# The triangular inversion of the heads on 32x32 diagonal blocks, with the work around it one level later

## The chip, the cores and the metric

The kernel runs on one core of a Trainium2 chip. It is written for the engines directly: TensorE (PE in the profile), VectorE (DVE), ScalarE (ACT), GpSimd (POOL) and SyncE (SP, which issues the DMAs) each run their own list of instructions in order and meet only through semaphores. The metric is the device time of one execution in microseconds. The kernel before takes 1651.7 us, the median of three runs (1651.15 to 1654.02).

## The reference, cut to what matters

The program is two transformer-like blocks. The change touches one part of the first: the gated delta rule, for 16 value heads in pairs that share a key head, 256 tokens in 4 chunks of 64.

```python
# per head and chunk of 64 tokens; g is a running sum of log decays
decay = jnp.exp(jnp.where(lower, g[..., :, None] - g[..., None, :], -jnp.inf))
L = jnp.where(strict, jnp.einsum('bhncd,bhnsd->bhncs', kb, k) * decay, 0.0)
T = lax.linalg.triangular_solve(eye + L, eye, left_side=True, lower=True, unit_diagonal=True)
u = T @ vb
w = T @ (kb * jnp.exp(g)[..., None])
attn = jnp.einsum('bhncd,bhnsd->bhncs', q, k) * decay
# scan over the chunks
v_new = u_n - w_n @ state
o = q_n @ state + a_n @ v_new
state = state * gl_n + k_n.T @ v_new
# then
o = rmsnorm(o, norm_w) * silu(z)
```

In the kernel a chunk has 128 tokens, so a head has two of them, and `T` is the inverse of a unit lower triangular 128x128 matrix.

## The kernel before, in words

The heads' stage is eight rounds (`GQ = 8`). A round handles one key head, that is two value heads `g`, each with two chunks: four 128x128 matrices are inverted in a round. All four engines run a function `inner(i, f, n)` per round: `i` is the round whose inverse is built, `f` the round before (its recurrence and output are finished in the gaps), `n` the next round (its keys, decays and lower matrices are set up in the gaps).

The inverse grows by doubling. After level `j` the diagonal blocks of size `2^(j+1)` are inverted; a level takes two neighbouring blocks and fills the square below them with `-X2 * L21 * X1`. PE does `level_p` (the product with `L`, line 2410; from level 1 on first a transpose of `X`, line 2406, for the next factor), DVE masks the result out of PSUM into `Pm` (`mask_level`, line 1641; 1638 in level 5), PE does `level_d` (line 2426; 2428 in level 5) and DVE subtracts (`close_level`, line 1652). ACT copies the transposed `X` back (`turned_over`, line 920). All products up to level 4 are over the full 128x128 matrices, whatever the block size, and separately for the two heads `g`; level 5 uses 64x64 products (lines 2413 and 2428). Six levels, 0 to 5, make a round. The start of `X` for the next round is a product of a mask and `L` on DVE (`starts_low` and `starts`, lines 1626 and 1632), transposed on PE (`setup_x0`, line 2385) and copied by ACT (line 938).

Between the levels stand, on PE, the steps 0 to 5 of `finish` (lines 2438 to 2458: the recurrence and output of `f`), `setup_keys` (2364 to 2369), `setup_rows` (2353), `setup_values` (2376), `norm_sums` (2337) and `modulator` (2395). The place of each is written out by hand in the four `inner` functions. `modulator` is something else: a 1 MB tile of `ada_w` (the next block's shift and scale) is loaded in each round into the raw slot 2, scaled and summed by POOL, and summed across partitions by PE.

Weights of the big projections go through four raw slots of 1 MB; ACT makes `w_hi` of a tile (line 738) and DVE `w_lo` (line 1378), in two slots. Right behind the rounds stands the output projection `a_w_out` (`T_AOUT`, line 2515), eight tiles in two halves of four. Its tiles 0 and 1 are loaded before the rounds, tile 2 after the last modulator, tile 3 only when the last output is done (`h_out`), because the raw slot 3 holds `XX`, `LT` and `BV` of the odd rounds.

On PE a plain product in f32 is two instructions in the trace, each a weight load (PEld) and a MATMUL (PE); a transpose is one.

Of the kernel before, what the change touches and what calls it, by code (L numbers as in the profile page):

```python
# [51 lines left out]
def program(nc, x, c, norm_w, ada_w, ada_b, a_w_in, a_conv_w, a_A_log, a_dt_bias, a_norm_w, a_w_out,  # L52
# [4 lines left out]
    with ctx:  # L57
# [112 lines left out]
        def pair(name):  # L170
            return [sem(f"{name}0"), sem(f"{name}1")]

        h_row, h_eg, h_dta, h_dt, h_lt, h_xt, h_xm, h_xT, h_x0, h_vT, h_bv, h_kd = (
            sem("h_row"), sem("h_eg"), sem("h_dta"), sem("h_dt"), sem("h_lt"), sem("h_xt"),
            sem("h_xm"), sem("h_xT"), sem("h_x0"), sem("h_vT"), sem("h_bv"), sem("h_kd"))
        h_p, h_pm, h_d, h_xx = sem("h_p"), sem("h_pm"), sem("h_d"), sem("h_xx")
        h_turn, h_turned = sem("h_turn"), sem("h_turned")
# [23 lines left out]
        MSUM = RAW[2][:, 0, :]  # L201
# [33 lines left out]
        def raw_count(base, i, u):  # L235

            n = base + u
            quads = 48 * ((n - T_WQ) // 4 + 1) if n >= T_WQ else 0
            gates = (0, 0, 16 * GQ, 0)[n % 4] if n >= T_AOUT else 0
            return 16 * i + (16 * (n // 4) + gates + quads)  # L240
# [80 lines left out]
        GBh, DT, KKb, LT, AT, QD, BV, XX, VN, S1h, KD, R1 = ([], [], [], [], [], [], [], [], [], [], [], [])  # L321
        for g_ in range(2):
            for lst, n in ((GBh, 512), (DT, 256), (KKb, 256), (LT, 256), (AT, 256), (QD, 128), (BV, 256),
                           (XX, 512), (VN, 256), (S1h, 128), (KD, 128), (R1, 128)):
                lst.append(temp(n))
        zeroed = at(2048 * (T_AOUT % 4), 2048, RAW01)
        Pm = [[(zeroed[:, 512 * j:512 * j + 512] if j < 4 else GBh[j - 4])[:, 256 * g_:256 * g_ + 256] for g_ in range(2)]
              for j in range(6)]
        LT, AT, QD, BV, XX, KD = [LT], [AT], [QD], [BV], [XX], [KD]
        SQ.append(GBh[0])  # L330
        RN.append(GBh[1])
# [8 lines left out]
        nm1T = LMASK[:, 0:128]  # L340
        lvl = [LMASK[:, 128 * (j + 1):128 * (j + 2)] for j in range(6)]
# [7 lines left out]
        XX.append([at(30720 + 512 * g_, 512) for g_ in range(2)])  # L349

        def left(ap, j, c):

            return ap.rearrange("p (c n h b) -> p c n h b", c=c, h=2, b=2 << j)[:, :, :, 0, :]

        LT.append([at(31744 + 256 * g_, 256) for g_ in range(2)])
        BV.append([at(32256 + 256 * g_, 256) for g_ in range(2)])
        A2 = [ps[0][:, 0:256], ps[1][:, 0:256]]
        A2_FIRST = [ps[2][:, 0:256], ps[3][:, 0:256]]
        B2 = [ps[0][:, 256:512], ps[1][:, 256:512]]
        ROWS = [ps[6], ps[7]]  # L360
        DIAG = two(at(26880, 256))
# [78 lines left out]
        def _(sp):  # L440
# [75 lines left out]
            for u in range(2):  # L516
                load(T_AOUT, 0, u, a_w_out[0, 0:D, :], TW * u)
            with sp.Fori(0, GQ) as i:
                sp.wait_ge(raw_free, i + (8 + N_ADA))
                sp.dma_start(RAW[2], ada_w[1][:, bass.ds(TW * i, TW)].rearrange("(k p) n -> p k n", p=P)).then_inc(raw_in[2], 16)  # L520
            sp.wait_ge(raw_free, 8 + N_ADA + GQ)
            load(T_AOUT, 0, 2, a_w_out[0, 0:D, :], TW * 2)
            for u, read, n in ((0, h_qd, GV), (2, h_vT, GV), (3, h_vT, GV), (1, h_s3, Round(GQ - 1).nth(1, 1, 2, 4))):
                sp.wait_ge(read, n)
                src = ada_w[1][:, 2 * D + TW * u:2 * D + TW * u + TW]
                sp.dma_start(GATEW[u], src.rearrange("(k p) n -> p k n", p=P)).then_inc(gate_in, 16)
            for kh in range(2):
                for u in range(3 if kh == 0 else 0, 4):
                    if kh == 0 and u == 3:
                        sp.wait_ge(h_out, 2 + GV)  # L530
                    load(T_AOUT + 4 * kh, 0, u, a_w_out[0, kh * D:(kh + 1) * D, :], TW * u)
# [69 lines left out]
        def _(pool):  # L601
# [30 lines left out]
            for j in range(6):  # L632
                b = 2 << j
                m = lvl[j].rearrange("p (n h b) -> p n h b", h=2, b=b)[:, :, 0, :]
# [4 lines left out]
            m = nm1T.rearrange("p (n h) -> p n h", h=2)[:, :, 1]  # L639
            keep(m, 0, [[-2, 64]], 1, -1.0, ALU.not_equal)  # L640
# [25 lines left out]
            for i in range(GQ):  # L666
                pool.wait_ge(raw_in[2], 16 * i + 16 * (T_AOUT // 4))
                for kk in range(KC):
                    pool.tensor_tensor(RAW[2][:, kk, :], RAW[2][:, kk, :], condT[:, kk:kk + 1].broadcast_to([P, TW]),
                                       ALU.mult).then_inc(mod_sum, 1)  # L670
                for half, done in ((4, 8), (2, 12), (1, 14)):
                    pool.wait_ge(mod_sum, 15 * i + (24 + done))
                    for kk in range(half):
                        pool.tensor_tensor(RAW[2][:, kk, :], RAW[2][:, kk, :], RAW[2][:, kk + half, :],
                                           ALU.add).then_inc(mod_sum, 1)
# [52 lines left out]
        def _(act):  # L728
# [167 lines left out]
            def setup_keys(r):  # L896
                act.wait_ge(g_k0, r.count(1, 1))
                act.activation(K0, ps[7][:, 0:128], ACT.Copy).then_inc(g_k0s, 1)
                if r.at:
                    act.wait_ge(h_at, r.count(2))  # L900
                act.activation(KQs, two(ps[7][:, 256:512]), ACT.Copy).then_inc(g_kqs, 1)
# [15 lines left out]
            def turned_over(r, j):  # L917
                for g in range(2):
                    act.wait_ge(h_turn, r.nth(g, 1, j - 1, 5))
                    act.activation(XX[r.side][g][:, 256:512], ps[3 + 2 * g][:, 256:512], ACT.Copy).then_inc(h_turned, 1)  # L920
# [13 lines left out]

            def setup_x0(r):
                for g in range(2):
                    act.wait_ge(h_xT, r.nth(g))
                    act.activation(XX[r.side][g][:, 0:256], (A2 if r.at else A2_FIRST)[g], ACT.Copy).then_inc(h_x0, 1)
# [29 lines left out]
            def inner(i, f, n):  # L968
                if f:
                    finish_first(f)  # L970
                turned_over(i, 1)
# [17 lines left out]
                if f:  # L989
                    finish_out(f)  # L990
# [1883 lines left out]
```

## Time and profile before

| | |
|---|---|
| median of the runs | 1651.7 us |
| the profiled execution | 1650.68 us, its span 1649.0 us |
| PE busy | 1594.5 us, 97% |
| DVE, ACT, POOL busy | 68%, 58%, 30% |
| the eight rounds, by the timeline | 198.4 to 360.5 us |
| behind them, the output projection | from 361.3 us |

A busy engine is one with an instruction under way. The profile models the ends of matmuls, so two matmuls that follow each other overlap in it, and the distance of their starts (the pitch) says more than their mean. Idle time is given with what ended it.

### The profile page before, as it was taken

What the parts mean: (1) busy time and instruction counts of PE and PEld (TensorE: products, weight loads), DVE (VectorE), ACT (ScalarE), POOL (GpSimd) and SP (SyncE); (2) the same over time, 40 slices, a digit from 0 to 9 for tenths busy, and PEclk for the clock granted to TensorE, in tenths of its full rate; (3) what the DMA queues carried; (4) which work ended last, traced back from release to release, by engine and by line L of the source; (5) the groups of instructions that cost most, each with busy time, mean ns of one, the idle gap of its engine ahead of it and who ended that gap; (6) DMA issues with size and microseconds to landing.
All of it is one profiled execution on the core that took longest, in us unless ns stands there. A gap on an engine that the chain in (4) does not pass through costs nothing.

```text
span 1649.0 us, 33605 instructions
## 1 busy us (share of the span) xinstructions
PE 1594.5 (97%) x11469; PEld 1482.8 (90%) x11477; DVE 1126.0 (68%) x2361; ACT 949.8 (58%) x1811; POOL 491.9 (30%) x406
## 2 busy tenths in 40 slices
PE   7999999999999999999999999999999999999998
PEld 6899899999898899889999999899999888888886
DVE  3787767755556574586469889889898555555554
ACT  1765566664465554563444444689898555544454
POOL 3000256647000005000037777766666100000000
PEclk9999999999999999999999999999999999999999
DMA  9668211138353245247535555554444556666553
GB/s 292 219 185 279 78 52 52 53 121 257 108 154 103 93 158 179 77 128 184 123 112 169 170 173 166 161 152 141 137 138 132 178 191 192 193 193 196 192 191 128
DMA packets 211818, 255.67 MB, mean 155 GB/s; under 512 B 15911, under 2 KB 193803, under 8 KB 211723
## 3 DMA queue, kind: packets, MB, share of 16 engines
q1 hardware_dynamic: 211723, 254.39, 50.5%
q8 instruction: 62, 1.02, 0.3%
q14 instruction: 33, 0.27, 0.1%
HBM read 253.29 MB, written 1.05 MB: 154 GB/s over the span
## 4 chain that ended last, share of the span: by engine, by line
PE 65%; issue 19%; POOL 9%; DVE 3%; ACT 2%; DMA 2%; SPq 1%; POOLq 0%; another core or an unknown queue 0%; DVEq 0%; ACTq 0%
PE ps L2825 21%; PE ps L2234 14%; PE ps L2807 9%; POOL w_lo L721 8%; PE ps L2795 3%; PE ps L2426 2%; PE ps L2515 2%; PE ps L2410 2%; PE ps L2254 1%; PE ps L2406 1%; DMA arena<-in_ada_w 1%; PE ps L2592 1%; POOL arena L711 0%; PE ps L2612 0%; PE ps L2329 0%
## 5 line engine op out<-in xcount | busy, mean ns | idle before, releaser
L721 POOL TENSOR_TENSOR w_lo<-raw,w_hi 128x1024 fp32r<-128x1024 f32 x128 | 307.6, 2407 | 331.7 <-ACT w_hi L1247 331.4
L2234 PE MATMUL ps<-x_hi,w_hi 128*128 128x256 f32 x1088 | 315.2, 290 | 8.1 <-DVE w_lo L1378 3.0
L2234 PE MATMUL ps<-x_lo,w_hi 128*128 128x256 f32 x1088 | 308.3, 283 | 0.0
L2234 PE MATMUL ps<-x_hi,w_lo 128*128 128x256 f32 x1088 | 308.2, 283 | 0.0
L2193 DVE TENSOR_TENSOR w_lo<-raw,w_hi 128x1024 fp32r<-128x1024 f32 x124 | 152.0, 1225 | 143.3 <-ACT w_hi L1356 143.3
L1356 ACT ACTIVATE w_hi<-raw 128x1024 fp32r<-128x1024 f32 x124 | 131.6, 1061 | 167.9 <-PE ps L2825 167.9
L2234 PEld LDWEIGHTS ps<-x_hi,w_hi 128*128 128x128 f32 x1088 | 209.0, 192 | 14.5 <-issue 5.8
L2234 PEld LDWEIGHTS ps<-x_lo,w_hi 128*128 128x128 f32 x1088 | 209.2, 192 | 1.3 <-issue 1.2
L2234 PEld LDWEIGHTS ps<-x_hi,w_lo 128*128 128x128 f32 x1088 | 209.0, 192 | 0.0
L1247 ACT ACTIVATE w_hi<-raw 128x1024 fp32r<-128x1024 f32 x128 | 134.9, 1054 | 110.3 <-DVE raw L1995 110.2
L2770 PE MATMUL ps<-x_hi,w_hi 128*128 128x256 f32 x576 | 165.1, 287 | 9.5 <-ACT arena L1269 8.2
L1995 DVE STREAM_TRANSPOSE raw<-raw 128x1024 f32<-128x1024 f32 x128 | 158.0, 1235 | 15.6 <-DMA raw<-in_u_experts 13.5
L2770 PE MATMUL ps<-x_lo,w_hi 128*128 128x256 f32 x576 | 162.8, 283 | 0.0
L2770 PE MATMUL ps<-x_hi,w_lo 128*128 128x256 f32 x576 | 162.7, 283 | 0.0
L2825 PE MATMUL ps<-w_hi,x_hi 128*128 128x512 f32 x512 | 157.7, 389 | 1.1 <-DVE x_lo L2183 1.1
L2825 PE MATMUL ps<-w_hi,x_lo 128*128 128x512 f32 x512 | 157.7, 389 | 0.0
L2825 PE MATMUL ps<-w_lo,x_hi 128*128 128x512 f32 x512 | 157.6, 389 | 0.0
L1378 DVE TENSOR_TENSOR w_lo<-arena,w_hi 128x2048 fp32r<-128x2048 f32 (+1 forms) x43 | 97.0, 2256 | 75.7 <-ACT w_hi L738 75.7
L1378 DVE TENSOR_TENSOR w_lo<-raw,w_hi 128x2048 fp32r<-128x2048 f32 (+1 forms) x43 | 97.0, 2255 | 64.1 <-ACT w_hi L738 64.1
L2807 PE MATMUL ps<-x_lo,w_hi 128*128 128x256 f32 x448 | 131.9, 294 | 0.0
L2807 PE MATMUL ps<-x_hi,w_hi 128*128 128x256 f32 x448 | 126.7, 283 | 0.0
L2807 PE MATMUL ps<-x_hi,w_lo 128*128 128x256 f32 x448 | 126.5, 282 | 0.0
(432 smaller groups left out, 3734.9 us busy)
## 6 DMA issues: line engine op xcount, KB each, us to landing
raw<-in_u_experts SPq DMA_DIRECT2D x512, 128.0 KB, 2.6
raw<-in_v_experts SPq DMA_DIRECT2D x128, 512.0 KB, 4.3
arena<-in_ada_w SPq DMA_DIRECT2D x22, 1024.0 KB, 7.8
raw<-in_a_w_in SPq DMA_DIRECT2D x12, 1024.0 KB, 5.8
arena<-in_a_w_in SPq DMA_DIRECT2D x12, 1024.0 KB, 5.5
raw<-in_b_w_in SPq DMA_DIRECT2D x8, 1024.0 KB, 5.5
arena<-in_b_w_in SPq DMA_DIRECT2D x8, 1024.0 KB, 5.5
raw<-in_w_in SPq DMA_DIRECT2D x8, 1024.0 KB, 5.4
```

The source lines that it names most:

```text
L721: pool.tensor_tensor(UTL[e], UT[e % 2], UTH[e].bitcast(F32), ALU.subtract).then_inc(utl_ready, 1)
L1247: act.activation(UTH[e % 4], UT[e % 2], ACT.Copy).then_inc(uth_ready, 1)
L1356: act.activation(VH[u], VRAW[u], ACT.Copy).then_inc(high_ready, 1)
L1378: v.tensor_tensor(WLO[:, slot, 0:k, :], RAW[raw_slot(base, u)][:, 0:k, :], WHI[:, slot, 0:k, :].bitcast(F32), ALU.subtract).then_inc(lo_re ...
L1995: v.transpose(UT[s_].rearrange("p (k a j) -> p a k j", k=KC, a=4), URAW[s_].rearrange("p (a k i) -> p a k i", a=4, k=KC)).then_inc(ut_read ...
L2193: v.tensor_tensor(VL[u], VRAW[u], VH[u].bitcast(F32), ALU.subtract).then_inc(low_ready, 1)
L2234: ins = mm(o[:, b * S:b * S + S], w[:, slot, kk, b * P:b * P + P], xx[:, (kk + turn) % KC, :], start=(kk == 0 and n == 0), stop=(kk == k - ...
L2410: ins = mm(A_[g][:, cc * 128:cc * 128 + 128], lt[:, cc * 128:cc * 128 + 128], xx[:, cc * 128:cc * 128 + 128], start=True, stop=True)
L2770: ins = mm(ps[e % 2][:, 0:S], w[e % 4][:, kk * P:kk * P + P], xx[:, kk, :], start=(kk == 0 and n == 0), stop=(kk == KC - 1 and n == 2))
L2795: ins = mm(GB.rearrange("p (e t) -> p t e", t=4)[:, q, :], OHJ[:, c % 2, q, :], OHI[:, c % 2, q, :], start=True, stop=True, skip_group_che ...
L2807: ins = mm(ps[e % 2][:, 0:S], w[e % 4][:, kk * P:kk * P + P], xx[:, kk, :], start=m == 0, stop=m == 23)
L2825: ins = mm(ps[4 + 2 * t + h][:, :], g[:, u, t * P:t * P + P], w[u][:, 512 * h:512 * h + 512], start=False, stop=False, skip_group_check=True)
```

## The change

Levels 0 to 3 work on the 32x32 diagonal blocks only. The four matrices' diagonal blocks are packed densely: `XC` is `[128, 4, 32]` (partition block `q` of matrix `m` holds that diagonal block), and its transpose `XC_T` is kept beside it by DVE's 32x32 block transpose. A product of a level is 16 small matmuls, one for each matrix `m` and each partition block `q` of 32, with one semaphore at the end for both heads; DVE masks 64 columns for all four matrices in one instruction and subtracts in one. Level 4 uses 32x32 products and writes its results by VectorE into `XPAIR` (64x64 blocks) and `INVT` (the transposed inverse); level 5 uses 64x64 products. ACT spreads the 32x32 blocks into `XPAIR` and `INVT` (`spread`, three parts of two copies). PE's transposes and ACT's copies of them are gone, and so is `setup_x0`; `setup_low` (16 small matmuls with the identity) takes its place. The steps of `finish` and the setup stand one place later. The modulator's tiles alternate between raw slots 2 and 0, the temporaries leave raw slots 1 and 3, and tile 3 of `a_w_out` is loaded before the rounds, tile 2 after the seventh modulator.

```diff
-            with sp.Fori(0, GQ) as i:
-                sp.wait_ge(raw_free, i + (8 + N_ADA))
-                sp.dma_start(RAW[2], ada_w[1][:, bass.ds(TW * i, TW)]...).then_inc(raw_in[2], 16)
+            sp.wait_ge(raw_free, 8 + N_ADA)
+            for i in range(GQ):
+                if i == 1:
+                    sp.wait_ge(lo_ready, tile_no(T_AOUT, 0, 0))
+                elif i:
+                    sp.wait_ge(raw_free, 8 + N_ADA + i - 1)
+                slot = MOD_SLOT[i % 2]
+                sp.dma_start(RAW[slot], ada_w[1][:, TW * i:TW * i + TW]...).then_inc(raw_in[slot], 16)
...
             def mask_level(r, j):
-                for g in range(2):
-                    v.wait_ge(h_p, r.nth(g, 1, j, 6))
...
-                    v.tensor_tensor(left(Pm[j][g], j, 2), left(ps[2 + 2 * g][:, 0:256], j, 2),
-                                    left(lvl[j], j, 1).broadcast_to([P, 2, n, b]), ALU.mult).then_inc(h_pm, 1)
+                v.wait_ge(h_p, r.count(6, j + 1))
+                if j < 4:
+                    n, b = 16 >> (j + 1), 2 << j
+                    mask = lvl[j].rearrange("p (n b) -> p n b", b=b).unsqueeze(1).broadcast_to([P, 4, n, b])
+                    v.tensor_tensor(dense(PC[:, 0:64], j), left(PA[:, 0:128].rearrange("p (m n) -> p m n", m=4), j),
+                                    mask, ALU.mult).then_inc(h_pm, 1)
...
             def close_level(r, j):
...
+                if j < 4:
+                    xx = left(XC, j)
+                    v.tensor_tensor(xx, xx, dense(PBC, j), ALU.subtract).then_inc(h_xx, 1)
+                    v.wait_ge(h_xx, r.count(12, 2 * j + 1))
+                    v.transpose(XC_T, XC).then_inc(h_xx, 1)
...
             def level_p(r, j):
-                        for cc in range(2):
-                            ins = pe.transpose(B_[g][:, 256 + cc * 128:384 + cc * 128], xx[:, cc * 128:cc * 128 + 128], ident)
-                        ins.then_inc(h_turn, 1)
-                    for cc in range(2):
-                        if j < 5:
-                            ins = mm(A_[g][:, cc * 128:cc * 128 + 128], lt[:, cc * 128:cc * 128 + 128],
-                                     xx[:, cc * 128:cc * 128 + 128], start=True, stop=True)
+                if j < 4:
+                    for m, q, g, at_ in diagonal_blocks():
+                        ins = mm(PA[q:q + 32, 32 * m:32 * m + 32], lt[g][q:q + 32, at_:at_ + 32], XC[q:q + 32, m, :],
+                                 start=True, stop=True)
...
             def level_d(r, j):
...
+                if j < 4:
+                    for m, q, g, at_ in diagonal_blocks():
+                        ins = mm(PBC[q:q + 32, 16 * m:16 * m + 16], XC_T[q:q + 32, m, :], PC[q:q + 32, 16 * m:16 * m + 16],
+                                 start=True, stop=True)
...
+            def diagonal_blocks():
+                return [(m, q, m // 2, 128 * (m % 2) + q) for m in range(4) for q in (0, 32, 64, 96)]
```

What PE has at the start of a round (the first two levels, with the steps 0 and 1 of `finish` for the round before), before and now:

```order
L2410 MATMUL ps<-arena 128x128 [waits h_x0]
L2438 MATMUL ps<-arena 128x128 [waits h_x0,h_bv,h_xx] x2
L2426 MATMUL ps<-raw,arena 128x128 [waits h_pm]
L2442 MATMUL ps<-arena 128x128 [waits h_kd,h_c3] x2
L2406 MATMUL ps<-small,arena 128x128 [waits h_xx]
L2410 MATMUL ps<-arena 128x128 x2
L2364 MATMUL ps<-arena 128x128 [waits h_bv,ada_free,g_norm]
```

```order
L2424 MATMUL ps<-arena 32x32 [waits h_xt]
L2424 MATMUL ps<-arena 32x32 x15
L2451 MATMUL ps<-arena 32x16 [waits h_xx,h_xt,h_pm]
L2451 MATMUL ps<-arena 32x16 x15
L2474 MATMUL ps<-arena 128x128 [waits h_bv,h_orn,h_spread,h_xx] x2
L2424 MATMUL ps<-arena 32x32 [waits h_xx]
L2478 MATMUL ps<-arena 128x128 [waits h_kd,h_c3] x2
L2381 MATMUL ps<-arena 128x128 [waits ada_free,g_norm]
```

The first step of `finish` stood between `level_p` and `level_d` of level 0 (line 2438 ahead of 2426); now nothing stands there (2451 right behind 2424), and it comes behind `level_d` (line 2474).

The end of a round on PE, now (levels 4 and 5, the last `finish` step 2494, `setup_low` 2402, the modulator 2410):

```order
L2429 MATMUL ps<-arena 32x32 [waits h_xx]
L2429 MATMUL ps<-arena 32x32 x7
L2456 MATMUL ps<-arena 32x32 [waits h_xx,h_pm]
L2458 MATMUL ps<-arena 32x32 x2
L2494 MATMUL ps<-arena,small 128x256 [waits h_sq] x2
L2402 MATMUL ps<-small,arena 32x32 [waits h_lt]
L2402 MATMUL ps<-small,arena 32x32 x15
L2434 MATMUL ps<-arena 64x64 [waits h_spread,h_xx]
L2410 MATMUL ps<-small,arena 128x1 [waits ada_free,mod_sum]
L2462 MATMUL ps<-arena 64x64 [waits h_spread,h_xx,h_pm]
```

Between `level_p` and `level_d` of level 4 (2429, 2456) nothing stands either; line 2494 stood there before.

## Rows read from the trace of the kernel before

**Rows 1.** The page: the span and PE's busy time.

```profile
span 1649.0 us, 33605 instructions
PE 1594.5 (97%) x11469; PEld 1482.8 (90%) x11477; DVE 1126.0 (68%) x2361; ACT 949.8 (58%) x1811; POOL 491.9 (30%) x406
```

**Rows 2.** Busy time by stretch: two middle rounds, the last but one, the last.

```profile
core 0: us, PE busy (x) PEld busy (x) DVE busy (x) ACT busy (x) POOL busy (x), PEclk, DMA share, GB/s
237.77:258.49 20.72, 20.67 (x173) 19.04 (x174) 15.20 (x44) 13.96 (x44) 12.79 (x19) 1.00 0.17 53
258.49:279.20 20.71, 20.66 (x173) 19.03 (x173) 15.19 (x44) 13.95 (x44) 12.90 (x19) 1.00 0.17 51
320.64:340.50 19.86, 19.81 (x172) 18.77 (x172) 15.17 (x44) 12.91 (x41) 12.90 (x19) 1.00 0.12 41
340.50:359.70 19.20, 17.75 (x153) 16.69 (x152) 11.42 (x32) 15.29 (x32) 11.69 (x15) 1.00 0.16 53
```

**Rows 3.** Groups by line in one round, 237.77 to 258.49 us.

```profile
L2410 PE MATMUL ps<-arena 128*128 128x128 f32 x40 | 6.0, 278 | 0.0
L920 ACT ACTIVATE arena<-ps 128x256 f32<-128x256 f32 x10 | 3.6, 388 | 1.3 <-PE ps L2406 1.3
L1652 DVE TENSOR_TENSOR arena<-arena,ps 128x128 f32<-128x128 f32 (+1 forms) x12 | 3.4, 285 | 3.6 <-PE ps L2426 2.1 <-PE ps L2428 1.5
L2426 PEld LDWEIGHTS ps<-raw,arena 128*128 128x128 f32 x32 | 4.0, 192 | 0.1
L2406 PE MATMUL ps<-small,arena 128*128 128x128 f32 x20 | 3.9, 277 | 0.0
L1641 DVE TENSOR_TENSOR raw<-ps,arena 128x128 f32<-128x128 f32 x8 | 2.2, 286 | 1.1 <-PE ps L2410 1.0
L1605 DVE TENSOR_TENSOR arena<-ps,arena 128x256 f32<-128x256 f32 x2 | 0.8, 420 | 0.4 <-ACT arena L908 0.4
```

**Rows 4.** Timeline: the end of a round and the start of the next.

```profile
256.31 0.44 PE L2406 MATMUL ps<-small,arena 128*128 128x128 f32 x2
256.67 0.44 PE L2413 MATMUL ps<-arena 64*64 64x64 f32 x4
257.05 0.65 PE L2385 MATMUL ps<-small,arena 128*128 128x128 f32 x4
258.49 0.54 PEld L2428 LDWEIGHTS ps<-arena 64*64 64x64 f32 x8 [0.76 <-issue]
258.49 0.68 PE L2428 MATMUL ps<-arena 64*64 64x64 f32 x8
260.43 0.97 PEld L2426 LDWEIGHTS ps<-raw,arena 128*128 128x128 f32 x8
```

**Rows 5.** Line 2428 and, 248 to 250 us, line 2452: durations, starts.

```profile
L2428 PEld LDWEIGHTS ps<-arena x64: 129/135/135, 217.1 to 360.4; 64*64 64x64 f32 x64
L2428 PE MATMUL ps<-arena x64: 218/218/267, 217.1 to 360.5; 64*64 64x64 f32 x64
...
L2452 PEldq EVENT_SEMAPHORE  x2: 51/51/51, 248.7 to 248.8; - x2
```

**Rows 6.** The page: VectorE's 32x32 block transpose elsewhere in the kernel.

```profile
L1995 DVE STREAM_TRANSPOSE raw<-raw 128x1024 f32<-128x1024 f32 x128 | 158.0, 1235 | 15.6 <-DMA raw<-in_u_experts 13.5
```

**Rows 7.** Timeline: PE's first steps of round 0.

```profile
197.42 0.44 PE L2385 MATMUL ps<-small,arena 128*128 128x128 f32 x2 [2.02 <-DVE arena L1632]
198.44 1.35 PE L2410 MATMUL ps<-arena 128*128 128x128 f32 x8
201.00 1.16 PE L2426 MATMUL ps<-raw,arena 128*128 128x128 f32 x8 [1.21 <-DVE raw L1641]
```

**Rows 8.** Behind the rounds: PE's wait (376 to 405 us), the chain, a stretch.

```profile
PE ps L2515 <- DVE w_lo L1378: 2.1, 1, 2.1
...
373.28 6.46 DMA arena<-in_a_w_out
...
384.60:388.00 3.40, 3.40 (x17) 3.40 (x18) 2.38 (x1) 0.09 (x1) 3.40 (x3) 0.50 1.10 348
```

More of the change, by code:

```diff
@@ L526, in _ @@
                 sp.dma_start(GATEW[u], src.rearrange("(k p) n -> p k n", p=P)).then_inc(gate_in, 16)
[L527 to L531, printed above, removed]
+            sp.wait_ge(raw_free, 8 + N_ADA + GQ)
+            for u in range(4):
+                load(T_AOUT + 4, 0, u, a_w_out[0, D:2 * D, :], TW * u)
             for n, tile_ in enumerate(B_ORDER):
@@ L1618, in lowers @@
                     v.wait_ge(h_dt, r.nth(g, 2))
[L1619 removed]
+                    v.wait_ge(h_xm, r.nth(g))
                     v.tensor_tensor(LT[r.side][g], KKb[g], DT[g], ALU.mult).then_inc(h_lt, 1)
[L1622 to L1626 removed]
@@ L1644, in close_level @@
-            def close_level(r, j):
-                for g in range(2):
-                    v.wait_ge(h_d, r.nth(g, 1, j, 6))
-                    if j == 5:
-                        xx = two(XX[r.side][g][0:64, 256:512])[:, :, 64:128]
-                        done = two(ps[3 + 2 * g][0:64, 0:256])[:, :, 0:64]
-                    else:
-                        xx, done = left(XX[r.side][g][:, 0:256], j, 2), left(ps[3 + 2 * g][:, 0:256], j, 2)
-                    v.tensor_tensor(xx, xx, done, ALU.subtract).then_inc(h_xx, 1)
+            def starts(r):
+                v.wait_ge(h_xT, r.count(1, 1))
+                v.tensor_tensor(XC, LOWC.rearrange("p (m n) -> p m n", m=4), bcast(nm1, 4), ALU.mult).then_inc(h_xt, 1)
+                v.wait_ge(h_xt, r.count(3, 1))
+                v.tensor_tensor(XC, XC, bcast(id32, 4), ALU.add).then_inc(h_xt, 1)
+                v.wait_ge(h_xt, r.count(3, 2))
+                v.transpose(XC_T, XC).then_inc(h_xt, 1)
@@ L1700, in inner @@
                 if n:
+                    betas(n)
+                close_level(i, 3)
+                mask_level(i, 4)
+                if n:
                     lowers(n)
@@ L2431, in finish @@
-            def finish(r, step, after=None):
+                lt = LT[r.side]
+                if j == 0:
+                    pe.wait_ge(h_xt, r.count(3, 2))
+                elif j < 5:
+                    pe.wait_ge(h_xx, r.count(12, 2 * j - 1))
+                else:
+                    pe.wait_ge(h_xx, r.count(12, 9))
+                    pe.wait_ge(h_spread, r.count(6, 2))
+                if j < 4:
+                    for m, q, g, at_ in diagonal_blocks():
+                        ins = mm(PA[q:q + 32, 32 * m:32 * m + 32], lt[g][q:q + 32, at_:at_ + 32], XC[q:q + 32, m, :],
+                                 start=True, stop=True)
+                elif j == 4:
+                    for m, q, g, at_ in diagonal_blocks():
+                        if q % 64 == 0:
+                            ins = mm(PA[q + 32:q + 64, 32 * m:32 * m + 32], lt[g][q:q + 32, at_ + 32:at_ + 64], XC[q:q + 32, m, :],
+                                     start=True, stop=True)
+                else:
+                    for m in range(4):
+                        at_ = 128 * (m % 2)
+                        ins = mm(PA[64:128, 64 * m:64 * m + 64], lt[m // 2][0:64, at_ + 64:at_ + 128], XPAIR[0:64, m, :],
+                                 start=True, stop=True)
```

309 lines of the change are left out of this document (155 added, 154 removed).

## The prediction

> **What bounds the kernel now.** I read the page first: PE is busy 97% of the span [rows 1], so PE's time counts nearly everywhere. Then the busy time by stretch over the rounds: a middle round takes 20.7 us and PE is busy for all of it; the last but one 19.9, the last 19.2 with 1.5 us idle [rows 2]. DVE is at 15.2 us of a round, ACT at 14.0, POOL at 12.9, the DMA share at 0.17. So the rounds are bound by PE's own instructions, and a change there is worth what it takes from or adds to PE's sum, the waits that it makes included. The groups by line give PE's counts, the timeline the pitch: eight weight loads of line 2426 take 0.97 us and the last 0.19 (the mean), so the pitch is 0.78 / 7 = 0.111 us for a 128x128 instruction; eight of line 2428, 64x64, take 0.54 and the last 0.135, a pitch of 0.058 [rows 3 to 5]. The pitch halves with the size but for some 4 ns: 64 columns less save 53 ns.
>
> **PE in a middle round, before.** Lines 2410, 2426 and 2406 are 40, 40 (32 in the row, 8 more in level 4) and 20 instructions [rows 3], line 2385 is 4 [rows 4]: 104 at 0.111 = 11.5 us. Levels 5 are 16 at 0.058 = 0.9. Changing between 128 and 64 costs too: from the start of the two transposes at 256.31 to the next 128x128 instruction at 257.05 are 0.74 us, where 2 at 0.111 and 4 at 0.058 make 0.45. That is 0.29 us for going there and back, three times a round (0.9). The rest, 20.7 - 13.3 = 7.4 us, is finish, keys, rows, values, sums and modulator, and stays.
>
> **PE in a middle round, after.** A level from 0 to 3 is 16 products for P and 16 for D, two instructions each: 4 x 64 = 256. Level 4 is 8 and 12 products (40 instructions), setup_low 16 (32). Together 328 small instructions; level 5 is 4 and 4 products, 16 instructions at 0.058 (0.9). No row shows a 32x32 instruction. From above it is bounded by the 64x64 one, 58 ns; from below by the issue: the two semaphore instructions of line 2452 start 0.1 us apart at the row's rounding, and between them in program order stand three products, six weight loads and six matmuls, so PE's sequencer gives out a pair in about 0.15 / 6 = 25 ns or less, and in a standing queue nothing excludes 12 [rows 5]. I take the value that continues the step from 111 to 58: halve 53 once more, 58 - 27 = 31 ns. 328 x 0.031 = 10.2 us.
>
> The round trips between sizes are now nine (finish 0, finish 1 with keys, finish 2, rows, finish 3, finish 4, values, finish 5, modulator with sums); at 0.29 less 0.03 for a shorter first weight load they cost 2.3, and two changes between 32 and 64 without return 0.2.
>
> New waits: between P and D of a level lies one dependent trip. The last matmul ends about 0.19 after its start (0.218 for 64x64 [rows 5]) instead of 0.03, the mask takes about 0.22 on DVE (0.42 for 256 columns of PSUM, 0.286 for 128 [rows 3]: 1.05 ns a column, so 64 columns 0.22), two semaphore steps some 0.1: 0.5 us. Between D and the next P it is the same with the subtraction. Before, the other head's products covered it; now both heads end with one semaphore. Where something stands in the gap it is covered (finish 0 to 3 are 4 x 0.111 + 0.26 = 0.7 us each, rows and values as much). Nothing stands between P and D of level 0 and of level 4: 1.0 us a round. The block transpose (1235 ns for 1024 columns [rows 6], so about 0.2 for 128) is needed only for D and lies beside P.
>
> Sum: 10.2 + 0.9 + 7.4 + 2.5 + 1.0 = 22.0 us, 1.3 more than 20.7. In six of the rounds (1 to 6): +7.8 us.
>
> In the last round nothing stands for the next: 296 small ones 9.2, 0.9, finish and modulator 4.3, seven trips 1.8 and 0.2, and four open gaps 2.0: 18.4 against 19.2, -0.8. In round 0 finish is missing: 10.2 + 0.9 + 3.1 + 1.3 + 3.0 (six open gaps) = 18.5; before, 19.3 from 198.44 to the next round's start, 1.2 of it the wait for DVE's memsets [rows 7]: -0.8.
>
> **The other engines.** DVE loses lines 1652, 1641, 1638, 1626, 1632 (about 9 us a round by the first two rows and their like) and gains some 5 us; ACT loses twelve copies of 0.388 (4.7) and gains six of about 0.28 (1.7). Neither becomes the bound at 22 us. The order on each was walked through: `normed` (2 x 0.6 us) before `close_level` 5 delays only D of level 0, one us later than it ends; `lowers` (1.2 us) stands before the closing of level 4, whose results PE needs after finish 5 and setup_low, 2 us later. `starts` waits for ACT's spreads, queued behind setup_v; behind it wait the level-5 mask and the modulator's copy; ACT is through with about 1 us to spare. If that cover is gone it costs 1 us a round. POOL's modulator (12.9 us a round) gets a second slot and stays hidden.
>
> **Ahead of the rounds.** PE waited 2.0 us for `starts_low` and `starts` [rows 7]. Now: lowers start 0.4 earlier (no memset before), low takes 1.0, two DVE operations 0.6, semaphores 0.2; the first P at about 197.2 instead of 198.4: -1.2.
>
> **Behind the rounds.** PE waits 2.1 us for `w_lo` of tile 3, whose DMA was issued at 373.28 when the last output was done, and took 6.46; right behind, for 3.4 us, the granted clock is 0.50, that is 1.2 instead of 2.4 GHz, after the wait: 1.7 us of work lost [rows 8]. Tiles 2 and 3 are now loaded long before, and the DMA queue of that stretch is 2 MB shorter. What is late next is tile 4 (its load now follows the gate tiles at about 364, needed at 388): hidden. -3.8 us; bounds 0 and -4.
>
> **Total.** 7.8 - 0.8 - 0.8 - 1.2 - 3.8 = +1.2 us. The profiled execution took 1650.7, its span 1649.0, and stands 1.0 below the median; 1650.7 + 1.2 = 1651.9, in terms of the median 1652.9. I forecast 1652: no change that can be told (a measurement of this kernel tells about 0.2%, 3.3 us).
>
> The sum hangs on the pitch: 328 x 8 = 2600 instructions, so each ns is worth 2.6 us. 58 ns give +70, 17 ns -37.
>
> **Rules against and for.** The row of line 2452 bears on a rule of the Trainium skill (TensorE: Matmul & The Clock Gate, section "Wait — 56ns, not 53.3ns?"): with hardware decode off the sequencer spends about 62 ns per matmul. Six matmuls would take 0.37 us, and the two semaphore instructions start 0.1 apart, so the trace speaks against it; by that rule alone the sum would be 328 x 31 ns = 10 us a round higher, 1733. The same section gives a floor of about 25 ns from start to start, by which the sum would be 16 us lower, an estimate from that page.
>
> **Rival 1: the blocks overlap (30%).** Consecutive small products use other partitions for input and output (q = 0, 32, 64, 96). If PE loads one block's weights while another's product runs, only the two instructions of one product stay in line, and a product costs about 31 + 4 ns: 17 ns an instruction. A round is then 22.0 - 328 x 0.014 = 17.4 us, with DVE and ACT near 13 still below it; eight rounds give -37, the time is 1616. For it: the order of the blocks makes it possible. Against: no product in this trace runs beside another. The Trainium skill (TensorEngine Tiling (Array Packing), section "Tiling Modes") says that different tiles load weights and multiply in parallel; no row here shows it.
>
> **Rival 2: a small instruction costs as much as a 64x64 one (16%).** Its place is the pair of weight load and matmul, 58 ns in line 2428. From about 33 ns on it makes the kernel slower by more than 0.2%; at 58 the rounds take 30.7 us and the time is 1722; at 40, 1676. For it: 58 is the shortest pitch of a pair in the trace. Against: it continues the line from 111 in proportion, as no floor would.
>
> **Rival 3: the clock (4%).** PE's gaps now come twice a level. If the granted clock fell to 1.2 GHz as after the 2.1 us wait [rows 8], PE's 21 us a round would double: over 1800. Against: 2.0 and 1.2 us of waits at 197 to 201 left it at full speed, and no gap here is over 1 us.
>
> **Rival 4: open gaps cost more (10%).** DVE's and ACT's queues close up and add 1 us in each round: 1661.
>
> **Chances.** The forecast's own case 40%, with a range of 1643 to 1662 for a pitch of 28 to 35 ns, both signs and no change about equally; rival 1 30%, rival 2 16%, rival 4 10%, rival 3 4%. Faster by over 0.2%: 0.30 + 0.15 = 0.45; within 0.2%: 0.16; slower 0.39. The range 1612 to 1678 takes in the overlap and pitches up to 40 ns; it leaves out the upper part of rival 2 and the clock.
>
> **What the changed profile would show.** The pitch of the 32x32 lines 2424 and 2451: 31 ns, a burst of 32 in 1.0 us; with overlap 0.55 us; with a floor 1.9. A round of 22 us with PE idle for 0.4 to 0.5 us twice (at lines 2451 in level 0 and 2456). PEclk at 1.00. No wait at line 2515 and no half clock behind the rounds. DVE and ACT at 12 to 13 us a round. I am wrong if a burst is much shorter or longer than 1.0 us, if PE waits for ACT's spreads, or if the stretch behind the rounds keeps its 3.8 us.

## The result, and the profile after

The changed kernel takes 1624.5 us (median of 4 runs, 1621.4 to 1628.8) against 1652.1 for the kernel before (1651.2 to 1654.0): ratio 0.983, 95% interval 0.981 to 0.986. In a second comparison on one chip it was 1624.3 (5 runs) against 1650.0, ratio 0.983 [0.982, 0.985]. I had forecast 1652 and no change; the kernel is 1.7% faster. The time is inside the range of 1612 to 1678, but the mechanism is not mine. It is that of rival 1, stronger than I had priced it, with part of the gain given back, so that the time lies inside the range is no merit of my sum.

The page of the changed kernel: span, PE, granted clock, instruction packets. These answer to [rows 1].

```profile
span 1619.6 us, 37025 instructions
PE 1554.8 (96%) x13269; PEld 1429.3 (88%) x13269; DVE 1109.9 (69%) x2304; ACT 932.7 (58%) x1763; POOL 493.4 (30%) x405
PEclk9999979899999999999999999999999999999999
q8 instruction: 76, 1.25, 0.3%
```

PE's time fell by 40 us, the span by 29.4. PEclk has a 7 and an 8 in the slices of the rounds, where the page of the kernel before has 9 throughout. The busy time by stretch (columns as in [rows 2]): round 1, round 2, a hole, a middle round, the last. Rounds are cut at the first product of line 2410.

```profile
209.13:228.75 19.62, 18.88 (x399) 14.70 (x398) 10.15 (x33) 10.69 (x35) 12.41 (x20) 0.72 0.18 56
228.75:244.08 15.33, 14.39 (x400) 11.24 (x398) 13.05 (x38) 11.80 (x39) 13.18 (x20) 1.00 0.23 72
244.08:260.67 16.59, 14.53 (x400) 11.35 (x398) 13.03 (x38) 11.79 (x39) 13.16 (x20) 1.00 0.20 66
260.67:275.95 15.28, 14.34 (x400) 11.23 (x398) 13.04 (x38) 11.79 (x39) 13.17 (x20) 1.00 0.24 73
306.51:325.82 19.31, 16.10 (x350) 13.42 (x348) 10.85 (x29) 12.91 (x30) 8.85 (x13) 0.65 0.67 217
```

Four of the middle rounds take 15.28 to 15.33 us, against 20.7 before [rows 2]. Round 1 and the last are 4 us longer, at a mean clock of 0.72 and 0.65. The trace has the half clock from 203.1 to 220.2 us (17.1 us, over rounds 0 and 1) and from 308.9 to 322.6 (13.7 us, in the last). Timeline of PE in a middle round, then the broken burst of the 16.59 us round:

```profile
277.45 0.68 PE L2462 MATMUL ps<-arena 64*64 64x64 f32 x8
278.05 0.45 PE L2424 MATMUL ps<-arena 32*32 32x32 f32 x32
279.05 0.44 PE L2451 MATMUL ps<-arena 32*32 32x16 f32 x32 [0.54 <-DVE arena L1653]
279.45 0.69 PE L2474 MATMUL ps<-arena 128*128 128x128 f32 x4
280.07 0.45 PE L2424 MATMUL ps<-arena 32*32 32x32 f32 x32
...
288.81 0.21 PE L2456 MATMUL ps<-arena 32*32 32x32 f32 x1 [0.39 <-DVE arena L1656]
```

```profile
250.22 0.37 PE L2451 MATMUL ps<-arena 32*32 32x16 f32 x22
251.72 0.29 PE L2451 MATMUL ps<-arena 32*32 32x16 f32 x10 [1.13 <-issue]
```

A burst of 32 takes 0.45 us, of which the last instruction is 0.19. From its first start to its last the trace has 263 ns, 263 / 31 = 8.5 ns from one to the next, where 64x64 instructions still stand 58 ns apart. The two open gaps are there as forecast, 0.54 and 0.39 us. Groups by line in the same round (what answers to [rows 3]):

```profile
L2424 PE MATMUL ps<-arena 32*32 32x32 f32 x128 | 1.8, 194 | 0.0
L1664 DVE TENSOR_TENSOR arena<-arena,ps 128x64 f32<-128x64 f32 x4 | 0.9, 218 | 1.3 <-PE ps L2451 1.3
L1653 DVE TENSOR_TENSOR arena<-ps,arena 128x64 f32<-128x64 f32 x4 | 0.8, 212 | 0.1
```

The mask and the subtraction on 64 columns take 0.21 and 0.22 us, as worked out from the wider ones. The hole of 1.13 us in the broken burst has no releaser: the burst stops after 22 of its 32. A second one, in the last round, is 0.3 us. The page counts 76 instruction packets, against 62 before, and the transfers of the trace speak for late instructions: a packet of 16 KB landed at 250.24 us, 1.5 us before the burst went on. In the profiles of this kernel and its edits below, PE has 34 such holes of 0.3 to 2.8 us in the rounds, and every one ends 1.2 to 1.6 us after a 16 KB instruction packet has landed. (Two kinds that recur at the same place with no such packet are left out: 0.33 us ahead of line 2372, and the one behind the last D, of which more below.)

By milestones in the two traces, after minus before: the first P is 2.1 us earlier (196.32 against 198.44 [rows 7]). The eight rounds, from there to the last D, take 130.1 us against 161.3 (-31.2), and from the last D to the end of the output projection the time is 2.0 shorter. That is -35.3. Then 2.8 us are lost at 650 us. These are the same instructions with the same wait ahead in both kernels, after and before:

```profile
650.79 0.80 PE L2628 MATMUL ps<-arena 128*128 128x128 f32 x2 [2.18 <-DVE arena L1828]
654.59 0.41 PE L2253 MATMUL ps<-x_lo,w_hi 128*128 128x256 f32 x1
```

```profile
686.06 0.49 PE L2592 MATMUL ps<-arena 128*128 128x128 f32 x2 [2.18 <-DVE arena L1809]
688.03 0.28 PE L2234 MATMUL ps<-x_lo,w_hi 128*128 128x256 f32 x1
```

Behind an equal wait of 2.18 us one execution fell to half clock (6.8 us long) and the other did not. The same wait stands in all eleven further profiles below, and ten of them fall there (for 3.4 or 6.8 us), only `no_gap` does not; with one profile of the kernel before, the record doesn't tell an effect of the change from chance. The remaining +3.2 us lie in the expert stretch, where PE waits 9.7 us for ScalarE instead of 8.2. That stretch differs by some us between the profiles of every kernel below, none of which touches it, and I don't put it down to the change.

### The profile page after: what moved, and what is told of

It is laid out like the page before. It is cut to its first block, busy times and chain, and to the rows that moved or that the text cites. A ratio compares the mean times of both kernels' runs of the same rounds, so it can differ in the third digit from the quotient of the medians.

```text
span 1619.6 us, 37025 instructions
## 1 busy us (share of the span) xinstructions
PE 1554.8 (96%) x13269; PEld 1429.3 (88%) x13269; DVE 1109.9 (69%) x2304; ACT 932.7 (58%) x1763; POOL 493.4 (30%) x405
## 4 chain that ended last, share of the span: by engine, by line
PE 72%; DVE 11%; issue 5%; DMA 4%; ACT 4%; SPq 2%; DVEq 0%; ACTq 0%
PE ps L2253 22%; PE ps L2861 22%; PE ps L2843 10%; PE ps L2831 3%; DMA raw<-in_u_experts 3%; PE ps L2273 2%; PE ps L2551 2%; DVE raw L2014 2%; SPq L580 2%; PE ps L2628 1%; DVE w_lo L1396 1%; PE ps L2451 1%; DMA arena<-in_ada_w 1%; DVE arena L2067 1%; PE ps L2648 1%
## 5 line engine op out<-in xcount | busy, mean ns | idle before, releaser
L2253 PEld LDWEIGHTS ps<-x_hi,w_hi 128*128 128x128 f32 x1088 | 209.1, 192 | 15.3 <-issue 6.0
L2014 DVE STREAM_TRANSPOSE raw<-raw 128x1024 f32<-128x1024 f32 x128 | 158.3, 1237 | 17.1 <-DMA raw<-in_u_experts 15.8
```

The costliest lines, as they stand in the source:

```text
L2014: v.transpose(UT[s_].rearrange("p (k a j) -> p a k j", k=KC, a=4), URAW[s_].rearrange("p (a k i) -> p a k i", a=4, k=KC)).then_inc(ut_read ...
L2253: ins = mm(o[:, b * S:b * S + S], w[:, slot, kk, b * P:b * P + P], xx[:, (kk + turn) % KC, :], start=(kk == 0 and n == 0), stop=(kk == k - ...
```

## Experiments

All are edits of the changed kernel. Unless said otherwise, the kernel before, run beside them on the same chip, took 1650 to 1651 us.

**Four products on one block in a row.**

```
-  return [... for m in range(4) for q in (0, 32, 64, 96)]
+  return [... for q in (0, 32, 64, 96) for m in range(4)]
```

> The changed kernel, but the 16 products of a burst stand in another order: four on the same 32 partitions in a row, then the next block, where they now go from block to block. Nothing is added. Theory (four blocks work beside each other: the profile of the changed kernel has a matmul every 8.5 ns in these bursts, about a quarter of the 31 ns that one 32-column instruction would take alone): the pitch goes to about 31 ns, a burst of 32 from 0.45 us to about 1.0 to 1.2 us, 288 such instructions a round cost 6.5 us more, the kernel is about 50 us slower than the changed one, near 1675 us, no better than before. Rival (a small product is simply cheap, wherever it lies): pitch and burst as they are, 1622 to 1629 us. Between them (two blocks in a row overlap only at the seams): 15 to 20 ns, 1640 to 1650 us.

1695.6 us, ratio 1.026 [1.023, 1.028]. Timeline at full clock, and the busy time of one round:

```profile
256.59 0.89 PE L2424 MATMUL ps<-arena 32*32 32x32 f32 x32
257.95 0.88 PE L2451 MATMUL ps<-arena 32*32 32x16 f32 x32
```

```profile
217.51:246.36 28.85, 27.82 (x397) 23.19 (x398) 9.71 (x33) 11.65 (x37) 9.89 (x16) 0.59 0.12 38
```

The burst goes from 0.45 to 0.89 us, a mean pitch of 22.7 ns. That mean mixes two things, which the single starts in the trace keep apart. Four of the 32 instructions last 212 ns, the others 191; I take these four for the first of each block, and they stand 153 to 154 ns apart. Read so, the instructions of one block start 52 and from then on 31 to 32 ns apart, and the next block begins 6 ns behind the fifth of the eight of the block before. So a block alone takes 31 to 32 ns for an instruction, and even in this order neighbouring blocks overlap for part of the time. The order alone doubles the burst, so the blocks do run beside each other.

It also costs 20 us more than expected. The pitch is worth 288 x 14.2 ns = 4.1 us a round, 33 us in all; most of the rest up to +71 goes with the clock, which is at half for some 150 us of the rounds. Idle time is not what takes it there, as this stretch at full clock shows, the last before a fall at 265.2 us:

```profile
254.95:265.15 10.20, 9.66 (x230) 8.31 (x230) 5.55 (x18) 6.77 (x24) 3.19 (x6) 1.00 0.02 3
```

PE is busy for 95% of it, while the middle rounds of the changed kernel kept their clock with 94% (14.34 of 15.28 us).

**Two blocks to and fro.**

```
+  return [... for h in (0, 64) for m in range(4) for q in (h, h + 32)]
```

> The changed kernel with the bursts' products going to and fro between two blocks of 32 partitions (0 and 32, then 64 and 96) instead of over four. Theory (blocks work beside each other, and each is taken for about 27 to 31 ns by one instruction): half the overlap, a pitch of 14 to 17 ns like the 16.6 ns of line 2429, which alternates between two blocks already; 288 instructions a round cost 2 us more, 16 us in all, more where the clock falls: 1640 to 1655 us. Rival (it is enough that the next product lies on another block, two are as good as four): 8.5 ns and the time of the changed kernel.

1634.1 us, ratio 0.990 [0.988, 0.991].

```profile
257.89 0.60 PE L2424 MATMUL ps<-arena 32*32 32x32 f32 x32
258.96 0.59 PE L2451 MATMUL ps<-arena 32*32 32x16 f32 x32
```

The mean pitch is 13.2 ns. Two blocks beside each other give 16, half of one block's 32, and the second pair begins before the first is through. With four blocks it is 8.5: a quarter of 32, and 53 instead of 32 ns from the first instruction of each block to its second. Line 2429, which alternated between two blocks at 16.6 ns, goes through one block and then the other in this order and takes 26.4 in the mean. A middle round is 16.7 us, 1.4 more than 15.3: 288 x 4.7 ns = 1.35. The time is lower than I expected because the pitch was.

**Every product of levels 0 to 3 twice.**

```
+  for _ in range(2):
       ins = mm(PA[...] / PBC[...], ...)
```

> The changed kernel with every product of levels 0 to 3 done two times in a row (256 more small instructions a round, the same result). Theory (8.5 ns each, issued without a hole): the bursts go from 0.45 to about 0.7 us and a round gets 2.2 us longer, eight rounds 17 us: 1641 us. If a product repeated on its own block has to wait for the first (the blocks overlap, but a block is busy for 31 ns): 31 ns each and +8 us a round, 1690 us. Rival (the burst is mostly latency that is hidden elsewhere): under 0.5 us a round, within 5 us of the changed kernel. Holes in which PE waits for its instructions should become more frequent if supply is near its limit: more than three of them over the rounds.

1678.9 us, ratio 1.019 [1.016, 1.021]. A burst and a round at full clock:

```profile
293.02 0.85 PE L2425 MATMUL ps<-arena 32*32 32x32 f32 x64
```

```profile
290.91:310.51 19.60, 17.70 (x655) 14.61 (x654) 13.04 (x39) 12.06 (x38) 13.27 (x20) 1.00 0.19 58
```

A burst of 64 takes 0.85 us, 10.4 ns each (a repeated product has to follow on its own block): eight bursts x 0.40 = 3.2 us more in the round. The round is 4.3 longer; 1.2 of that are "issue" holes (1.0 and 0.2). So neither price that I gave holds: the pitch was too low in the first, and 31 ns far too high in the second, since the other blocks still run beside it. Holes are 13 in the rounds, 14.6 us in all, against 2 and 1.4 us in the changed kernel; I had expected more than three if supply is near its limit. Five of the seven rounds behind the first show a clock of 0.54 to 0.85. Holes and clock together make the rest up to +54 us. Instruction packets are 92, that is 16 more for some 2,040 more matmuls and as many weight loads, about 255 instructions in each.

**The fourth output tile loaded late again.**

```
-  for u in (0, 1, 3):
+  for u in (0, 1):
...
+  sp.wait_ge(h_out, 2 + GV)
+  load(T_AOUT, 0, 3, a_w_out[0, 0:D, :], TW * 3)
```

> The changed kernel, but the last tile of the first half of the output weights is loaded where it was before the change, when the last head's output is done. Theory (its early load is what shortened the stretch behind the rounds): PE waits about 2 us at line 2515 for w_lo of tile 3 again, some us of half clock may follow, and the time from the start of the output projection to its end grows from 53.3 us by 2 to 4 us; the whole kernel is 2 to 4 us slower, 1626 to 1629 us with the clock as in the changed kernel. Rival (the shorter stretch comes from the other loads and from the clock): no wait, the end of the projection within 0.5 us.

1623.7 us, ratio 0.984 [0.982, 0.985]: in the total no difference to the changed kernel. Waits of PE from the rounds' end on, here (line 2553 is 2551 of the changed kernel) and in the changed kernel:

```profile
PE ps L2553 <- DVE w_lo L1398: 2.0, 2, 1.5
```

```profile
PE ps L2551 <- DVE w_lo L1396: 0.9, 1, 0.9
PE ps L2551 <- DVE x_lo L1405: 0.3, 1, 0.3
```

The stretch of the output projection takes 53.8 us instead of 51.3: 0.8 by the waits, and 1.7 by 3.4 us of half clock at 331.4, which may or may not come (the changed kernel's second profile has it too, without this edit). What these profiles leave to the early load itself is the 0.8 us.

**Idle products in all gaps.** Products of 128x128 with the identity, two at a time (three in a few places), in the two open gaps of each round, and in all gaps of the first and last.

```
+  def fill(bank, n=2):
+      keep_clock(ps[bank][:, 384:512], n)
```

> The changed kernel with idle products put on PE where its bursts wait for VectorE: 128x128 products with the identity into unused columns, two or three at a time, in the gap behind level_p of level 0 and of level 4 in each round, and in all gaps of the first and last round. Theory (the half clock at 203 to 220 us and at 309 to 323 us comes from PE being idle in these gaps): granted clock 1.00 over both stretches, rounds 0, 1 and 6, 7 at 15 to 16 us, together about 8 us less; against it the fillers cost where they run longer than the gap, up to 0.2 us a round: 1613 to 1619 us. Rival (the clock falls for the sum of the work or by chance, not for gaps): half clock in the same places or elsewhere, 1622 to 1632 us. The 3 us at 650 us, which no filler touches, stay.

1622.9 us, ratio 0.983 [0.982, 0.984]. The first half-clock stretch is gone (1.00 from 72 to 311 us) and round 1 takes 16.7; the one in the last round stays (10.2 us, then 3.4). Each middle round costs 0.57 us more:

```profile
242.57:258.42 15.85, 15.40 (x406) 12.33 (x406) 13.17 (x38) 11.81 (x39) 13.05 (x20) 1.00 0.21 69
```

Two fillers are 0.44 us and going to full size and back some 0.3 more, which doesn't fit into gaps of 0.54 and 0.39. The clock theory was half confirmed, the sum not.

**Big fillers or small ones, at the ends only.** Both kernels have idle products only in the first round, in the last, and before the last D of the last but one. One uses 128x128 products, the other five 32x32 products on one block for each of them.

```
+  def fill(i, bank, n):
+      if i.at in (0, GQ - 2, GQ - 1):
+          keep_clock(ps[4 if i.at == GQ - 1 else bank][:, 384:512], n)
or
+          for _ in range(5 * n):
+              mm(ps[...][0:32, 384:416], ident[0:32, 0:32], ident[0:32, 0:32], ...)
```

> The changed kernel with idle 128x128 products against the identity in the first round, before the last D of the last but one, and in the last round only: in the open gaps and, two to five at a time, where the setup of a next head or the finish of a last one is missing; the middle rounds are untouched. Theory (TensorE's clock falls there because too little of the array is at work, not because PE has gaps): with full-size products between the bursts the granted clock is 1.00 from 195 to 329 us, round 1 takes 15.3 us as the middle rounds do and the last 14 to 15.5 us, against 19.6 and 19.3; the fillers cost about 1 us in round 0. The rounds end 6 to 8 us earlier than in the changed kernel, the kernel takes 1614 to 1620 us. Rival (what the clock does there is chance, or is set by DVE and ACT or the loads of the last round): half clock stays in one of the two places, and the time is 1622 to 1630 us.

> As the kernel with fillers at both ends of the rounds, but each idle 128x128 product is replaced by five idle 32x32 products on one block (by the pitches of 22.7 and 111 ns about the same time on PE). Theory (the clock goes by how much of the array is at work): PE is as busy as with the big fillers and the clock falls all the same, at both ends, for 15 us or more each; 1630 to 1640 us. Rival (the clock goes by PE's idle time): 1.00 over both ends and the same time as with the big fillers, within 2 us.

Big: 1621.2 us, ratio 0.981 [0.980, 0.983], between what theory and rival gave. Small: 1639.4, ratio 0.994 [0.992, 0.996]. The same stretch, 200.2 to 230.9 us, with big fillers and with small ones:

```profile
200.20:230.90 30.70, 28.08 (x766) 22.72 (x766) 20.45 (x63) 19.46 (x63) 25.77 (x40) 1.00 0.19 59
```

```profile
200.20:230.90 30.70, 29.85 (x619) 25.76 (x620) 10.94 (x35) 10.01 (x32) 17.39 (x27) 0.50 0.12 37
```

With small fillers PE is busy for 97% of it and the clock is at half throughout; with big ones it is busy for 91% and the clock is full. The 97% are read at half clock, where each product takes longer, so what PE did before the fall counts for more. From 194.1 to 200.1 us, still at full clock, it was busy for 5.32 us with small fillers, for 5.92 with big ones and for 3.97 in the changed kernel. The clock fell at 200.2 us with small fillers and at 203.1 without any. With `same_block` above this says that PE's idle time alone is not what takes the clock, and that filling with the wrong kind makes it worse. The last round was not cured in the profiled execution of either: in both the clock falls at 319 us for 17 us, with big fillers behind this:

```profile
315.92 0.26 PE L2424 MATMUL ps<-arena 32*32 32x32 f32 x7
318.06 0.39 PE L2424 MATMUL ps<-arena 32*32 32x32 f32 x25 [1.89 <-issue]
```

A burst stops after 7 instructions and goes on 1.9 us later. (With small fillers a hole of 2.8 us comes only behind the fall.) An instruction packet of 16 KB is under way from 315.55 to 316.76, amid weight loads that move 350 GB/s. Other executions with big fillers had a mean clock up to 0.998, against 0.992 in the profiled one.

**TensorE's order as before, for the steps of finish.**

```
   level_p(i, 0)
+  finish(f, 0)
   level_d(i, 0)
+  finish(f, 1)
   level_p(i, 1)
   ...
   level_p(i, 4)
+  finish(f, 5)
   level_d(i, 4)
```

> The changed kernel with TensorE's order alone changed: the first, second and last step of finish stand one place earlier (0 between P and D of level 0, 1 behind D of level 0, 5 between P and D of level 4), as before the change for 0 and 5, so that no gap between P and D is open. ScalarE and VectorE keep their order. Theory A (the two open gaps of 0.5 and 0.4 us that a middle round has in the profile are the price of the later order): a round loses them and takes 14.4 to 14.8 us, the kernel is 4 to 6 us faster, 1618 to 1621 us. Theory B (the next queue is as late: step 1 then waits for ScalarE's copy of step 0's result, and behind D of level 4 setup_low waits for lowers on VectorE, 1.2 us long): a round takes 15.1 to 15.8 us and the time is within 3 us of the changed kernel.

1622.6 us, ratio 0.982 [0.981, 0.984]: theory B by the time, and the round says why (busy time of a middle round, then PE's waits in it):

```profile
263.44:278.85 15.41, 14.45 (x399) 11.31 (x398) 12.39 (x38) 11.81 (x39) 13.43 (x20) 1.00 0.22 72
```

```profile
PE ps L2474 <- DVE arena L1674: 0.6, 1, 0.6
```

15.41 against 15.28. Both open gaps are closed, and finish 0 now waits 0.6 us for the closing of level 5 on VectorE (line 1674), which stands behind `normed` there. My expectation had named other waits for it. The later order is worth 0.1 us a round; it is not where the gain comes from.

**The changed kernel again, filled in the first round only, and lightly at both ends.** Three kernels beside each other on one chip.

```
+  if i.at == 0:                        # first round only
+  if i.at in (0, GQ - 2, GQ - 1):      # both ends
+      keep_clock(..., 2)
```

> The changed kernel itself, unedited, run beside the next two so that their medians can be compared on one chip. Expected: 1621 to 1629 us, half clock in rounds 0 and 1 and in the last round.

> The changed kernel with idle 128x128 products, two at a time, ahead of the first burst and in the first round only. Theory (the first round lacks the finish products, so small bursts and gaps follow each other and the clock falls): full clock from 195 to 300 us, rounds 0 and 1 together 3 to 4 us shorter, the last round as in the changed kernel; the kernel is 3 to 4 us faster than the changed one on the same chip. Rival (the fillers cost in round 0 what they give back in round 1): within 1 us.

> The same with two idle products at a time at both ends (the kernel with big fillers had three to five, and PE spent 4 us on them in the last round). Theory: full clock at both ends in most executions, as there, and 2 to 3 us less of filling: 2 to 3 us faster than the kernel filled in the first round only, 1615 to 1619 us. Rival (the last round loses its clock to a hole in PE's instruction supply, 1.9 us in the profile of the kernel with big fillers, which no filler closes): half clock stays in the last round and the kernel is no faster than the one filled in the first round only.

Changed kernel 1624.3 us (1621.1 to 1625.6), ratio 0.983 [0.982, 0.985]. First round only 1619.7 (1617.5 to 1621.7), 0.981 [0.979, 0.982]. Both ends, lightly, 1619.9 (1619.5 to 1625.0), 0.982 [0.980, 0.984]. Rounds 1, 2 and the last of the kernel filled in the first round only:

```profile
209.47:225.32 15.85, 14.55 (x400) 11.30 (x398) 10.11 (x35) 10.58 (x35) 13.70 (x22) 1.00 0.21 70
225.32:240.65 15.33, 14.39 (x400) 11.28 (x398) 13.04 (x38) 11.84 (x39) 13.19 (x20) 1.00 0.23 72
301.94:321.31 19.37, 15.96 (x351) 13.35 (x349) 10.84 (x29) 12.91 (x30) 8.84 (x13) 0.65 0.67 217
```

Round 1 takes 15.85 us at full clock instead of 19.62, and round 0 ends at 209.47 us, between 209.13 and 209.63 in the two profiles of the changed kernel. The last round is untouched. The medians of this kernel and the changed one differ by 4.6 us and the runs barely meet, though the intervals of the ratios overlap: this is the lowest median of all versions, by a margin at the edge of what five runs tell. Filling the last round as well brings nothing more: it takes 21.2 us there at a clock of 0.76, where the unfilled one has 19.4 at 0.65, and its clock falls at 309.3 us, at the end of a hole of 0.75 us.

## Why the prediction was wrong

**The step that failed: "I take the value that continues the step from 111 to 58: halve 53 once more, 58 - 27 = 31 ns."** The pitch is 8.5 ns. As the time of an instruction alone on its block the value is right: `same_block` has 31 to 32 ns there (52 behind the first). What failed is the next line, "328 x 0.031 = 10.2 us", which puts all small instructions one behind the other; the kernel's order goes over four blocks, and four run at a time. With one, two and four blocks in turn the mean pitch is 22.7 (31 to 32 inside a block), 13.2 and 8.5 ns. My own bound from the issue ("nothing excludes 12") allowed nearly that. Having written that each ns is worth 2.6 us, I should have let the range of the pitch choose the likeliest case, not a line through two sizes that stand in line on their blocks. 2600 x 22.5 ns = 58 us is the size of the error.

**Rival 1** had the mechanism ("the order of the blocks makes it possible") and mis-sized its term: it let only a neighbour overlap, 17 ns. Its total of 1616 is nearer to the time than mine only because the deeper overlap is nearly cancelled by the lost clock, the holes and the dearer trips. (Rival 2's round at 58 ns adds up to 30.9 us, not 30.7; nothing hangs on it.)

**What the three orders say of the two rules.** Their pitches of 22.7, 13.2 and 8.5 ns agree with what the Trainium skill says (TensorEngine Tiling (Array Packing), section "Tiling Modes"): different tiles load weights and multiply in parallel. The Trainium skill also gives a floor of about 25 ns from start to start (TensorE: Matmul & The Clock Gate, section "Wait — 56ns, not 53.3ns?"). The 31 to 32 ns inside one block stay above it, but the pitch of 8.5 ns between blocks goes far below it, and the measurement decides.

**The rest of a middle round.** My 22.0 us less 328 x 22.5 ns are 14.6; measured 15.28. A trip from small products to full size and back is 0.13 behind the burst and 0.18 behind the four products (279.05 to 280.07 in the timeline above), 0.31 instead of 0.26: nine times 0.05 = 0.45. Level 4 works with fewer blocks at once, 16.6 ns at line 2429 and 0.37 us for its D: 0.3 more. The open gaps are 0.93 instead of 1.0. That makes 15.3. DVE and ACT are at 13.0 and 11.8 us, as I said. No wait for ScalarE's spreads is in it, and line 2462 waits once in all rounds, 0.7 us in the last, for DVE (line 1658).

**The clock (rival 3) was given 4% and came in part.** "No gap here is over 1 us" was the wrong argument: `same_block` and the kernel with small fillers show that busy time doesn't protect the clock when much of it is spent on 32x32 products, nor do gaps of half a microsecond cost it where full-size products stand between (the middle rounds). Before the change the last round was busy for 92% with 128x128 products and kept 1.00 [rows 2]. In the rounds 30.7 us are at half clock, which costs at most 15.4 us. For round 1 alone it is 4.3 us (19.62 against 15.33), and 3.8 of them came back with the fillers.

**Instruction supply** was in no case of mine: 1.4 us of holes in the rounds. No run was made to test the cause; it rests on the times of the packets, and on the 13 holes with doubled products.

**Ahead of the rounds** -2.1 instead of -1.2. PE's last wait there is still one for DVE (line 1644, 1.1 us).

**Behind the rounds** -2.0 instead of -3.8. The half clock of [rows 8] is gone (1.7), and the wait of 2.1 us went down to 0.9 for `w_lo`, plus 0.3 for `x_lo`; before the first product of finish there is a new wait of 0.86, for which the profile names no releaser. It fits DVE's closing of level 5 (line 1674), which now stands behind `normed`, runs from 327.44 to 327.85 us and ends 0.1 us before PE goes on; where `no_gap` has this wait in a round, the profile names that line. I had called what is late next "hidden"; it was not. I read it so that the rounds end 33 us earlier and DVE's splitting of the tiles has had that much less time; no run tests that.

**The sum again**, for the eight rounds: 161.3 before; my terms make it 167.5; less 58.5 for the pitch, plus 0.7 x 8 for trips and level 4 = 114.6; holes 1.4, half clock up to 15.4: up to 131.4, measured 130.1. How the clock's loss splits over the rounds to a microsecond stays open, and so does why one execution falls to half clock behind 2.18 us of waiting and another does not.

## What to carry to other kernels

When a product is cut into blocks on the diagonal, ask first in which order the blocks are issued: going over all four partition groups made the same 32 instructions take 0.45 us instead of 0.89, and it is one line. A term that 2600 instructions multiply must be priced by its bounds, and overlap between neighbours belongs into them. Where small products replace big ones, read the granted clock round by round: the first and the last round lost it here, where part of the full-size work between the bursts is missing, and the middle rounds lost it too once the bursts took twice as long. Two idle full-size products in each gap of the first round gave back 3.8 us of the next, while the same in the middle rounds cost 0.57 us each.

## What the runs showed of the hardware

- fp32 32x32 instructions: 31 to 32 ns apart on one block (52 to 53 from the first to the second). Means of a burst of 32: 22.7 ns one block after the other, 13.2 over two in turn, 8.5 over four; at half clock 36.0, 20.9 and 13.4. A product with 16 columns has the same pitch as one with 32 (lines 2451 and 2424).
- A burst of small instructions can break off for 0.3 to 2.8 us and goes on 1.2 to 1.6 us after a 16 KB instruction packet has landed (34 holes): 1.13 us in the changed kernel, 1.89 with 350 GB/s of loads beside it, 2.4 in the doubled kernel with 35 GB/s. Packets were 62, 76 and 92 for 11,469 matmuls before, 13,269 after and 15,309 with the doubled products.
- PE busy for 95% of 10.2 us at full clock, with bursts of 0.88 us of small products, and then a fall to half (`same_block`). Busy for 91% of 30.7 us with more full-size products between, and no fall (big fillers).
